# Attention by score rows: exponentials, the third head's products and the spare transposes at other steps of a block

## What is computed

```python
HEAD_DIM, N_Q, N_KV, Q_BLOCK = 128, 8, 2, 128

def _attend(q, k, v):
    s = jnp.einsum('btkgd,bskd->bkgts', q, k).astype(jnp.float32) * (HEAD_DIM ** -0.5)
    p = jax.nn.softmax(s, axis=-1).astype(v.dtype)
    return jnp.einsum('bkgts,bskd->btkgd', p, v)

    # in the odd layer, after the norms and rotary positions of q and k
    qb = jnp.moveaxis(q_lat.reshape(Bn, nb, Q_BLOCK, N_KV, Q_PER_KV, HEAD_DIM), 1, 0)
    o = lax.map(lambda qi: _attend(qi, k_all, v), qb)
    o_lat = jnp.moveaxis(o, 0, 1).reshape(Bn, L, C_WIDTH)
    x = x + gt * ((o_lat * jax.nn.silu(gate[:, n_ctx:])) @ w_out)
```

## Time and profile before

| | us |
|---|---|
| median of the runs | 1271.1 |
| the profiled execution's own time | 1269.24 |
| its span | 1267.3 |
| TensorE busy | 1180.9 (93%) |
| TensorE weight loads busy | 977.0 (77%) |
| VectorE busy | 800.0 (63%) |
| ScalarE busy | 506.9 (40%) |
| GpSimd busy | 174.3 (14%) |
| granted TensorE clock, mean | 0.989 of full speed |

### The profile page before, as it was taken

One profiled execution on the slowest core, in us unless ns is written; L12 is line 12 of the kernel. 1 busy time (PEld: TensorE's weight loads), 2 busy tenths in 40 slices (PEclk: granted clock), 3 DMA queues, 4 the chain that ended last, 5 costly groups with the idle time before them and its releaser, 6 DMA issues.

```text
span 1267.3 us, 17430 instructions
## 1 busy us (share of the span) xinstructions
PE 1180.9 (93%) x6962; PEld 977.0 (77%) x6962; DVE 800.0 (63%) x1423; ACT 506.9 (40%) x922; POOL 174.3 (14%) x154
## 2 busy tenths in 40 slices
PE   3899899999999899999999999989999999999997
PEld 2678788888889857877888878867777777777885
DVE  5798829799816263147649792247777777776127
ACT  3535456210016231144334331555665555555012
POOL 4700000000000003333112111100030000000232
PEclk9999999999999999999999999999999999999999
DMA  9834766335421952213022022112000000000413
GB/s 343 326 109 152 180 195 230 135 127 189 165 85 61 355 198 54 67 67 133 1 67 67 28 64 84 34 58 84 9 18 9 17 9 18 9 18 1 166 34 133
DMA packets 81024, 129.86 MB, mean 102 GB/s; under 512 B 12944, under 2 KB 43024, under 8 KB 80144
## 3 DMA queue, kind: packets, MB, share of 16 engines
q1 hardware_dynamic: 71120, 113.96, 26.8%
q10 hardware_dynamic: 9824, 14.80, 3.4%
HBM read 97.81 MB, written 30.93 MB: 102 GB/s over the span
## 4 chain that ended last, share of the span: by engine, by line
PE 67%; DVE 16%; ACT 8%; issue 5%; DMA 3%; POOL 1%; ACTq 0%; DVEq 0%
PE ps L1814 9%; PE ps L1816 9%; PE ps L1815 9%; PE ps L1676 5%; PE ps L1825 5%; PE ps L1826 5%; PE ps L1827 5%; DVE w_lo L1619 4%; DVE small L1580 3%; ACT w_hi L714 3%; PE ps L1973 2%; PE ps L2149 2%; PE ps L2151 2%; PE ps L2150 2%; ACT region_d L714 2%
## 5 line engine op out<-in xcount | busy, mean ns | idle before, releaser
L1814 PE MATMUL ps<-w_hi,a_hi 128*128 128x512 f32 x448 | 177.5, 396 | 6.8 <-DVE b_lo L1179 4.4
L1815 PE MATMUL ps<-w_lo,a_hi 128*128 128x512 f32 x448 | 175.6, 392 | 0.0
L1619 DVE TENSOR_TENSOR w_lo<-ps,w_hi 128x512 fp32r<-128x512 f32 x160 | 110.5, 691 | 75.7 <-ACT w_hi L714 72.5
L1816 PE MATMUL ps<-w_hi,c_lo 128*128 128x512 f32 x368 | 143.3, 389 | 0.0
L1825 PE MATMUL ps<-a_hi,w_hi 128*128 128x512 f32 (+1 forms) x384 | 138.4, 360 | 1.4 <-ACT region_d L714 1.4
L1826 PE MATMUL ps<-b_lo,w_hi 128*128 128x512 f32 (+1 forms) x384 | 136.3, 355 | 0.0
L1827 PE MATMUL ps<-a_hi,w_lo 128*128 128x512 f32 (+1 forms) x384 | 136.2, 355 | 0.0
L1580 DVE TENSOR_REDUCE small<-ps 128x1 f32<-128x1024 f32 (+1 forms) x128 | 103.6, 820 | 39.9 <-PE ps L2100 39.2
L714 ACT ACTIVATE w_hi<-ps 128x512 fp32r<-128x512 f32 x160 | 95.2, 596 | 76.7 <-PE ps L1676 73.3
L1814 PEld LDWEIGHTS ps<-w_hi,a_hi 128*128 128x128 f32 x448 | 85.0, 190 | 26.7 <-issue 7.9
L1815 PEld LDWEIGHTS ps<-w_lo,a_hi 128*128 128x128 f32 x448 | 85.0, 190 | 17.4
(11 more groups left out here) (229 smaller groups left out, 2465.0 us busy)
## 6 DMA issues: line engine op xcount, KB each, us to landing
weight_ring<-in_w_mod SPq DMA_DIRECT2D x10, 2048.0 KB, 9.1
weight_ring<-in_we_in SPq DMA_DIRECT2D x10, 1024.0 KB, 5.7
weight_ring<-in_wo_in SPq DMA_DIRECT2D x10, 1024.0 KB, 5.1
weight_ring<-cop_t_scratch SPq DMA_DIRECT2D x4, 1536.0 KB, 7.8
region_c<-in_w_mod SPq DMA_DIRECT2D x2, 2048.0 KB, 20.8
bop_scratch<-region_d ACTq DMA_DIRECT2D x16, 256.0 KB, 3.0
cop_t_scratch<-region_d SPq DMA_DIRECT2D x8, 512.0 KB, 7.6
weight_ring<-bop_scratch SPq DMA_DIRECT2D x2, 2048.0 KB, 9.7
```

The lines of the kernel that those rows point to most:

```text
L1619: v.tensor_tensor(p_lo[:, m % NP], ps[:, pt_bank(pt("tile", i, t)), :], p_hi[:, m % NP].bitcast(F32), ALU.subtract).then_inc(s_a_pt, 1)
L1814: te.matmul(o, th, wh[:, k % 4], start=k == 0, stop=False)
L1815: te.matmul(o, th, wl[:, k % 4], start=False, stop=False)
L1816: last = te.matmul(o, tl, wh[:, k % 4], start=False, stop=k == KT - 1)
```

## The change

Five things get another step. Q goes from step 3 to 4, with CQ and LQ. R goes from step 7 to 8, with G. S2b and S3a with their maxima go from step 4 to 5. The exponentials go from steps 1, 2, 4, 7 to 1, 3, 5, 7. The high copy of an output goes from step 5 to 6. The number of instructions is the same, and so are their shapes. The turn of the two banks changes with the places of Q and R: T0 to T4, Q, T5 to T8, R, T9 instead of T0 to T3, Q, T4 to T7, R, T8, T9. The same number replaces 7 by 8 in four other tests of VectorE, TensorE and the DMA queue's wait before a gate load; they are left out below.

```diff
         pt_order = [(kind, i, t) for i in range(NB) for t in range(TT) for kind in ("tile", "query", "sums")
-                    if kind == "tile" or (kind, t) == ("sums", 7) or ((kind, t) == ("query", 3) and i + 2 < NB)]
+                    if kind == "tile" or (kind, t) == ("sums", 8) or ((kind, t) == ("query", 4) and i + 2 < NB)]
...
         def scores_at(t):
-            return {0: [(0, 0), (0, 1)], 1: [(1, 0)], 2: [(1, 1), (2, 0)], 4: [(2, 1), (3, 0)], 6: [(3, 1)]}.get(t, ())
+            return {0: [(0, 0), (0, 1)], 1: [(1, 0)], 2: [(1, 1), (2, 0)], 5: [(2, 1), (3, 0)], 6: [(3, 1)]}.get(t, ())
...
-                if t == 3 and i + 2 < NB:
+                if t == 4 and i + 2 < NB:
                     act.wait_ge(s_a_qT, i + 3)
-                    q_round(i + 2, pt_bank(pt("query", i, 3)))
-                if t == 5 and i:
+                    q_round(i + 2, pt_bank(pt("query", i, 4)))
+                if t == 6 and i:
                     output_round(i - 1)
-                if i + 1 < NB and t in (1, 2, 4, 7):
-                    exponentials(i + 1, (1, 2, 4, 7).index(t))
+                if i + 1 < NB and t in (1, 3, 5, 7):
+                    exponentials(i + 1, t // 2)
...
-                if t == 3 and i + 2 < NB:
-                    q_rest(i + 2, pt_bank(pt("query", i, 3)), s_a_pt)
-                if t == 7:
+                if t == 4 and i + 2 < NB:
+                    q_rest(i + 2, pt_bank(pt("query", i, 4)), s_a_pt)
+                if t == 8:
                     gate_over_sums(i)
...
-                if t == 3 and i + 2 < NB:
-                    n = pt("query", i, 3)
+                if t == 4 and i + 2 < NB:
+                    n = pt("query", i, 4)
                     pt_free(n)
                     q_transposes(i + 2, pt_bank(n))
-                if t == 7:
+                if t == 8:
                     over_sums(i)
```

More of the change, by code:

```diff
@@ L549, in _ @@
                 if i >= 2:
-                    sp.wait_ge(s_a_pt, pt("sums", i - 2, 7) + 1)
+                    sp.wait_ge(s_a_pt, pt("sums", i - 2, 8) + 1)
                 if i == 3:
@@ L1596, in gate_over_sums @@
                 dve.wait_ge(s_a_rt, i + 1)
-                v.tensor_tensor(GR, gbuf[:, i % 2], ps[:, pt_bank(pt("sums", i, 7)), :], ALU.mult).then_inc(s_a_pt, 1)
+                v.tensor_tensor(GR, gbuf[:, i % 2], ps[:, pt_bank(pt("sums", i, 8)), :], ALU.mult).then_inc(s_a_pt, 1)
             def output(i):
@@ L1601, in output @@
                 dve.wait_ge(s_a_v, TT * (i + 1))
-                dve.wait_ge(s_a_pt, pt("sums", i, 7) + 1)
+                dve.wait_ge(s_a_pt, pt("sums", i, 8) + 1)
                 v.tensor_tensor(OT[:, b, HPK * kv:HPK * kv + HPK, :], GR.rearrange("p (h q) -> p h q", q=P),
@@ L2085, in scores @@
                     pe.wait_ge(s_a_qh, i + 1)
-                    pe.wait_ge(*((s_a_ql, i + 1) if i < 2 else (s_a_pt, pt("query", i - 2, 3) + 1)))
+                    pe.wait_ge(*((s_a_ql, i + 1) if i < 2 else (s_a_pt, pt("query", i - 2, 4) + 1)))
                 if part and n:
@@ L2132, in over_sums @@
                 pe.wait_ge(s_a_ri, i + 1)
-                n = pt("sums", i, 7)
+                n = pt("sums", i, 8)
                 pt_free(n)
```

## The result

| | before | changed |
|---|---|---|
| median of five runs, us | 1270.8 | 1278.64 |
| ratio, 95% interval | | 1.0072 (1.0049 to 1.0095) |
| profiled execution, us | 1269.24 | 1272.3 |
| its span, us | 1267.3 | 1270.4 |
| block of attention, us | 21.27 | 21.83 |

The changed kernel is slower by 0.72%, at 1278.64 us where 1279.8 were forecast.

The account below looks back on a forecast made before the run. TensorE's issue (19.0 us of a 21.27 us block) plus 2.27 of waits released by L was taken to bound the kernel. 8.3 + 0.45 gave 8.7 us on 1269.24, 1277.9; with 1.9 to the median, 1279.8, range 1274.5 to 1284.5.

Parts of the forecast that it names:

- Step 3: Attention block, step 3: C3 no longer behind E1, T4 follows V0 without its 1.55 us wait; gain so far 1.9 us.
- Step 4: Attention block, step 4: C4, ready at 1018.26, goes in only at 1018.95, 1.32 us behind E1's start.
- Copy to exponential: ScalarE handover from a copy to a ready exponential, not in the trace: taken as 0.50 us, between 0.47 and 0.69.
- Step 5: Attention block, step 5: T5 has T4's bank and needs L4, so TensorE waits 1.22 us; T4's wait moved here.
- Step 6: Attention block, step 6: E2 lets C6 in at 1024.27; S3b needs E2's end: no wait, or under 0.1 us.
- rival 3: Slower by more: third wait at S3b, for E2's end and sum; 1284.3 us with 0.3 beyond 0.5; chance 0.08.
- Steps 8 and 9: Attention block's end: E3 lets C8 in 1.32 us later; T9 has T8's bank, needs L8 and waits 1.47 us.
- The block: One attention block, walked: ends at 1030.07 instead of 1029.48, 0.59 us longer; waits 2.87 instead of 2.27.
- The sum: Whole kernel: fourteen blocks at 0.59 (8.3 us), block 0 at 0.45, block 15 at 0; sum 8.7 us.
- Rival 1: Faster: E3 is out of the way before C8 is due at the block's end; 5.1 us less, 1266.0; chance 0.08.
- Rival 2: No difference: holds at C4 and C8 each 0.3 us shorter than walked; 1268.6 to 1273.6 us; chance 0.08.
- The term for block 0: Block 0, M2b behind the values' low part: both orders hold E3 alike; between 0.3 and 0.6, charged 0.45 us.

## Why the prediction was right, step by step

- **Step 3, T4's wait goes.** Right: T4 starts 1.13 behind T3.
- **Step 4, C4 behind E1.** Right: C3, E1 and C4 are each at 0.49 and 1.30 from the one before, walked 0.50 and 1.32. Copy to exponential, the price that no row had shown, lies near the lower of its bounds (0.47 and 0.69).
- **Step 5, the wait at T5.** 1.20 against 1.22.
- **Step 6, S3b under 0.1.** It starts 0.05 late, and its first product then takes 0.22 to the next one and not 0.12, so T7 comes 1.65 behind T6, where T6 to T7 took 1.48 before: 0.17 instead of the 0.08 in the walk. It costs nothing, since T9's wait takes it up, as rival 3 says of small waits at S3b.
- **Steps 8 and 9, C8 behind E3 and the wait at T9.** 1.40 against 1.47, with R 0.06 later than walked. Moving E3 away takes 0.86 us off the block, and 0.47 us more behind E3 puts 0.50 on: the chain from E3 to T9 is on the path one for one.
- **The block.** From T3 to T0 block 8 takes 1029.05 - 1015.47 = 13.58 us, against 12.99 before: 0.59, as walked. (The waits of before add up to 2.26, not 2.27, and T3 to V0 is 0.36 in the earlier trace rows, not 0.35; neither moves the walk.)
- **The sum** is closer than its parts, and that is luck. From T0 of block 1 to T0 of block 15 it is 1155.52 - 859.28 = 296.2 us before and 1158.54 - 854.41 = 304.1 changed: 7.9 us for fourteen blocks, 0.56 each, where I had 8.3. Block 0, from the last gate product to T0 of block 1, took 859.28 - 834.0 = 25.3 us before and 854.41 - 828.2 = 26.2 changed: 0.9 more, where I had 0.45. Block 15 costs nothing, as said. The two misses nearly cancel.
- **Rival 1** came true only once E3 was moved. With E3 at step 8, T9 starts 2.01 behind T8, the sum of the three prices in the rival, and the kernel is faster than before. The Trainium skill ("Perfetto Trace Analysis", Optimization Strategy) advises to make what a gap waits for start sooner. Here C3, which T4's gap waited for, did start 1.03 sooner, and the block became longer, because another copy, C4 behind E1, became what a gap waits for.
- **Rival 2** needed an exponential that lets the next copy in after 1.0: in both kernels it is 1.30 to 1.32 wherever that copy was ready.
- **Rival 3** did not come true in the change, but its mechanism did where the exponentials were moved alone.

The term for block 0 was the one of wrong size, 0.9 where the sum has 0.45. I had argued that both orders hold E3 by the values' low part alike. They don't hold S3b alike. In block 0 of the changed kernel M2b stands behind that low part, so E2 starts only at 846.95, and S3b, due at 846.41, starts at 848.42. The second row is T0 of block 1, its first two transposes:

```profile
848.42 0.39 PE L2098 MATMUL ps<-k_t_hi,q_t_hi 128*128 128x256 f32 x1 [1.85 <-ACT region_c L1026]
...
854.41 0.38 PE L1676 MATMUL ps<-ident,region_b 128*128 128x128 f32 x2
```

Before, S3b doesn't wait there. With S2b and S3a back at step 4 and all else as changed, block 0 takes 856.40 - 831.8 = 24.6 us, so it is their place that costs. Behind the wait the granted clock was 0.54 from 848.9 to 852.4 us in this execution; how much of the 0.9 is the wait and how much the clock isn't taken apart.

## What to carry to other kernels

Where two banks go round between engines that each keep their own order, look for the transpose that has only a spare transpose, and no long products, between its bank's last filling and itself. Follow its low part and its copy back, and ask what stands in front of that copy on its engine. Put the long instruction behind the copy that is needed soonest (E3 behind C8: 0.86 us a block less), and put a spare transpose in front of long products (Q in front of S1b and S2a: 0.87 less). Price such edits together, in a walk over one block from start to start: the prices of three parts alone are 0.55, 0.79 and -0.01, in sum 1.33, and the change that holds them and a fourth part cost 0.56.

## What was not expected of the hardware

TensorE's wait for an exponential with a sum ended when the sum was read out, a step of 0.19 to 0.20 us of its own behind the exponential: S3b starts 0.05 us behind the end of that read in two kernels (E2 + 1.47 changed, E2 + 1.46 with the exponentials alone).

The last gate product, the end of the untouched part, started between 828.2 and 838.5 us in the thirteen profiled executions. In the pair before and changed, 3 to 4 of the 5.8 us come from one place. Two windows of before, then the same two of the changed kernel (TensorE busy is the first number, the clock the third from the end, then the DMA share):

```profile
155.00:160.00 5.00, 1.94 (x46) 1.11 (x40) 3.24 (x3) 0.84 (x2) 0.00 (x0) 0.86 1.03 368
160.00:165.00 5.00, 5.00 (x25) 3.93 (x18) 1.07 (x6) 2.35 (x5) 0.00 (x0) 0.80 0.47 188
```

```profile
155.00:160.00 5.00, 5.00 (x38) 4.04 (x37) 2.60 (x8) 2.36 (x5) 0.00 (x0) 1.00 1.04 419
160.00:165.00 5.00, 5.00 (x32) 4.37 (x31) 1.33 (x1) 3.31 (x4) 0.00 (x0) 1.00 0.16 66
```

Before, TensorE waits there 3.06 us, and the granted clock is 0.50 from 158.6 to 161.6, 1.2 instead of 2.4 GHz: the products behind the wait follow each other at 0.43 us instead of 0.23. In the changed kernel's execution the wait at the same instruction is 0.61 us and the clock stays at 1.00. The DMA share is full during both waits (1.00 and 1.03), and the row names no releaser, so the cause stays open. A difference of 0.7% should therefore be read from the stretch that the change touches, and the whole time only from several runs.
